# A hybrid decoder step in fp32: the SSD chunks' weight-times-value products and the token sums, each as two products of 64 stationary columns

## The reference, cut to what matters

```python
wgt = cbw[..., None] * lmask * dtb[:, None]
y = jnp.einsum('bijgr,bjgrp->bigrp', wgt, xb)          # per head: 128 tokens x 128 tokens, times 128 x 64
y = y + jnp.einsum('bign,bgrpn->bigrp', cb, s) * jnp.exp(cum)[..., None]
```

```python
y = xf * lax.rsqrt(jnp.mean(xf * xf, axis=-1, keepdims=True) + EPS)
```

## Time and profile before

| what | before |
|---|---|
| median of 3 runs | 2888.15 us (2887.59 to 2888.18) |
| profiled execution, its own time | 2894.47 us |
| its span | 2892.7 us |
| TensorE busy (PE) | 2830.8 us, 98% of the span |
| DVE, ACT, POOL busy | 58%, 20%, 35% |
| mean granted TensorE clock | 0.988 of full speed |

### The profile page before, as it was taken

The page is one execution under the profiler, slowest core; times in us unless marked ns, Lnnn a source line. Parts: engine busy times, 40 slices in busy tenths (PEclk is TensorE's granted clock), DMA queues, the critical chain, the costliest instruction groups (busy, mean ns, idle before and its releaser), DMA issues.

```text
span 2892.7 us, 46994 instructions
## 1 busy us (share of the span) xinstructions
PE 2830.8 (98%) x18230; PEld 2770.3 (96%) x18230; DVE 1667.6 (58%) x2116; ACT 589.2 (20%) x902; POOL 1020.8 (35%) x440
## 2 busy tenths in 40 slices
PE   9999999989999999999999999998999999999997
PEld 8999999989999999999999999998899999999997
DVE  7659786366444444444746597855664444444447
ACT  4333231113100011100323332211221110111102
POOL 2333233213344343443433333231144343443432
PEclk9999999999999999999999999999999999999998
DMA  4315324411111111111123334344011111111112
GB/s 157 129 67 165 119 99 163 133 53 38 52 44 48 47 44 51 44 48 46 56 89 100 119 123 145 108 140 140 31 46 44 51 44 51 44 44 51 44 51 86
DMA packets 76113, 228.08 MB, mean 79 GB/s; under 512 B 18704, under 2 KB 19728, under 8 KB 74912
## 3 DMA queue, kind: packets, MB, share of 16 engines
q1 hardware_dynamic: 71600, 210.79, 22.3%
q10 hardware_dynamic: 4368, 15.33, 1.8%
HBM read 180.63 MB, written 45.96 MB: 78 GB/s over the span
## 4 chain that ended last, share of the span: by engine, by line
PE 87%; issue 6%; DVE 5%; DMA 1%; POOL 1%; ACT 1%; DVEq 0%; SPq 0%; POOLq 0%; ACTq 0%
PE ps L696 27%; PE ps L698 26%; PE ps L697 26%; DVE sb_pt L1503 2%; PE ps L808 1%; PE ps L866 1%; DMA sb_w_raw<-w 1%; PE ps L810 1%; PE ps L929 1%; DMA sb_raw<-proj 0%; PE ps L813 0%; PE ps L930 0%; POOL sb_w_hi L675 0%; PE ps L974 0%; DVE sb_y_lo L1882 0%
## 5 line engine op out<-in xcount | busy, mean ns | idle before, releaser
L696 PE MATMUL ps<-sb_h_hi,sb_w_hi 128*128 128x344 f32 x3840 | 1244.0, 324 | 6.7 <-DVE sb_ev L1490 3.7
L697 PE MATMUL ps<-sb_h_lo,sb_w_hi 128*128 128x344 f32 x3840 | 1230.6, 320 | 0.0
L698 PE MATMUL ps<-sb_h_hi,sb_w_lo 128*128 128x344 f32 x3840 | 1230.1, 320 | 0.0
L675 POOL TENSOR_TENSOR sb_w_hi<-sb_w_raw,sb_ones 128x1024 fp32r<-128x1024 f32 x218 | 424.5, 1947 | 1813.3 <-PEq L693 861.5
L696 PEld LDWEIGHTS ps<-sb_h_hi,sb_w_hi 128*128 128x128 f32 x3840 | 726.2, 189 | 16.6 <-issue 7.5
L697 PEld LDWEIGHTS ps<-sb_h_lo,sb_w_hi 128*128 128x128 f32 x3840 | 726.2, 189 | 1.0
L698 PEld LDWEIGHTS ps<-sb_h_hi,sb_w_lo 128*128 128x128 f32 x3840 | 726.1, 189 | 0.0
L678 POOL TENSOR_TENSOR sb_w_lo<-sb_w_raw,sb_w_hi 128x1024 fp32r<-128x1024 f32 x218 | 596.1, 2734 | 17.1
L696 PE MATMUL ps<-sb_y_hi,sb_w_hi 128*128 128x344 f32 x1440 | 476.3, 331 | 20.7 <-DVE sb_x L1493 14.4
L698 PE MATMUL ps<-sb_y_hi,sb_w_lo 128*128 128x344 f32 x1440 | 465.4, 323 | 0.0
L697 PE MATMUL ps<-sb_y_lo,sb_w_hi 128*128 128x344 f32 x1440 | 462.7, 321 | 0.0
(11 more groups left out here) (266 smaller groups left out, 2256.4 us busy)
## 6 DMA issues: line engine op xcount, KB each, us to landing
sb_w_raw<-w SPq DMA_DIRECT2D x222, 512.0 KB, 3.6
proj<-sb_ev SPq DMA_DIRECT2D x64, 516.0 KB, 3.1
sb_pt<-proj SPq DMA_DIRECT2D x28, 516.0 KB, 5.1
sb_raw<-proj SPq DMA_DIRECT2D x16, 516.0 KB, 4.5
sb_raw<-proj ACTq DMA_DIRECT2D x16, 516.0 KB, 4.3
sb_ch<-cumT SPq DMA_DIRECT2D x32, 256.0 KB, 4.1
sb_raw<-ssd_state SPq DMA_DIRECT2D x4, 1024.0 KB, 6.4
o_ssd_s<-sb_ch SPq DMA_DIRECT2D x4, 1024.0 KB, 3.9
```

The source lines that it names most:

```text
L675: nc.gpsimd.tensor_tensor(w_hi[:, q, :], w_raw[:, q, :], ones[:, 0:1].to_broadcast([P, 1024]), ALU.mult).then_inc(sg.sem("w_hi_done"), 1)
L696: mm(o, wh, ah, start=first, stop=False)
L697: mm(o, wh, al, start=False, stop=False)
L698: return mm(o, wl, ah, start=False, stop=last)
```

## The change

Each 128-column stationary block of these products is halved. Where a product wrote 128 partitions of PSUM, there are now two: the first 64 stationary columns write partitions 0 to 63 and the other 64 write partitions 64 to 127, of the same bank and column. Both stream the same moving operand. The ninth product, that of the 8 sample tokens, stays one. No wait, buffer or transfer changes; the signal of the token sums still comes from the last product. In the "mix" call the early signal `w_used1` comes after the second half of the first block.

```diff
         def token_sums(key, freed=None):
 
-            for c in range(NCH + 1):
-                s = slice(c * CHUNK, min((c + 1) * CHUNK, T))
-                ins = mm(ps[0:s.stop - s.start, 7, c:c + 1], rstd[:, s], ones[:, 0:1], start=True, stop=True)
+            for c in range(NCH):
+                for n in range(2):
+                    s = slice(c * CHUNK + 64 * n, c * CHUNK + 64 * n + 64)
+                    ins = mm(ps[64 * n:64 * n + 64, 7, c:c + 1], rstd[:, s], ones[:, 0:1], start=True, stop=True)
                 if c == 0 and freed:
                     ins.then_inc(sg.sem(freed), 1)
-            ins.then_inc(*sg.on("tok_sum", key))
+            mm(ps[0:DEC, 7, NCH:NCH + 1], rstd[:, d], ones[:, 0:1], start=True, stop=True).then_inc(*sg.on("tok_sum", key))
@@
             for h in range(4):
-                mm(ps[:, 6, 64 * h:64 * h + 64], W(c)[:, 128 * h:128 * h + 128], xdt(c)[:, 64 * h:64 * h + 64],
-                   start=True, stop=True)
+                for n in range(2):
+                    mm(ps[64 * n:64 * n + 64, 6, 64 * h:64 * h + 64], W(c)[:, 128 * h + 64 * n:128 * h + 64 * n + 64],
+                       xdt(c)[:, 64 * h:64 * h + 64], start=True, stop=True)
@@
-        for c in range(NCH + 1):
-            s = slice(c * CHUNK, min((c + 1) * CHUNK, T))
-            ins = mm(ps[0:s.stop - s.start, 3, c:c + 1], ev[:, 1, s], ones[:, 0:1], start=True, stop=True)
-        ins.then_inc(*sg.on("tok_sum", "last"))
+        for c in range(NCH):
+            for n in range(2):
+                s = slice(c * CHUNK + 64 * n, c * CHUNK + 64 * n + 64)
+                mm(ps[64 * n:64 * n + 64, 3, c:c + 1], ev[:, 1, s], ones[:, 0:1], start=True, stop=True)
+        mm(ps[0:DEC, 3, NCH:NCH + 1], ev[:, 1, d], ones[:, 0:1], start=True, stop=True).then_inc(*sg.on("tok_sum", "last"))
```

## The result

The changed kernel took 2894.44 us (median of 20 runs, 2889.79 to 2896.20), the kernel before, beside it on the same chip, 2887.74 us (20 runs, 2884.25 to 2893.90). The ratio is 1.0019, with a 95% interval of 1.0013 to 1.0025: slower by 5.5 us (3.8 to 7.2), where 7.2 us of gain had been forecast. The two medians lie 6.7 us apart; the text goes by the ratio and its interval.

A forecast was written before the change was run, and what follows sets the result against it. TensorE, busy 98% of the span, was taken to bound the kernel. Gains of 4.6 (SSD steps) + 1.3 ("ffn") + 0.6 ("mix") + 0.7 (end) = 7.2 us gave 2881.0 us, range 2877.0 to 2885.8.

The forecast's parts named there:

- the one on "mix": Token sums of the "mix" calls: nothing arrives in the first layer, 0.64 us arrive in the second.
- The waits themselves should stay: SSD steps: TensorE's waits for DVE's last step or W(c) remain, because DVE starts on both from TensorE's earlier signal.
- SSD steps: Line 808's 32 steps: 0.07 us gained in each of 20 without a wait, 0.27 in 12 with one; 4.6 us.
- Every sign of being right: Expected timings at the changed products, about 12 waits as before, first "mix" spreading at about 42.93, last near DVE's reciprocal.
- "ffn": Token sums of the "ffn" calls, both layers: a projection product follows directly, so 2 x 0.64 = 1.3 us arrive.
- Of being wrong: Half loads spaced 0.055 us without overlap, longer SSD waits for DVE, or low-clock stretches changed by more than two.
- A pair of halves, the passage in: Halves load beside each other: sixteen loads take 0.62 us, and going from whole blocks to halves costs 0.25 us.
- The end: Last set of sums, line 1086: the final spreading starts earlier, at about 2874.0; gain 0.7 us, bounds 0 and 0.8.
- The rival on the clock: Clock falls come or go as work moves, 1.4 us each; two give 2878.2 or 2883.8 us; chance 0.28.
- serial halves: Halves load one after the other, so a round costs 0.11 us, not 0.06; 2898 us, 0.35% slower; chance 0.04.
- slow streams: Costlier passage in or halves' streams taking turns: sixteen loads 0.73 us or more, gain at most 3.7 us; chance 0.10.
- The rival that DVE takes the SSD gain: DVE sets the pace of SSD chunks, so line 808's waits grow; 2.6 us left, 2885.5 us; chance 0.10.

The follow-up runs named there:

- before_s32: The kernel before with 8 small products (8x8) added behind the warm-up and no halves anywhere; 2896.75 us, 1.0026 of the kernel before.
- after_w12: The changed kernel with a warm-up of 12 products of 208 columns in place of 20 of 128; 2886.59 us, 0.9993 of the kernel before.

## Why the prediction was wrong

The step that failed is the one on "mix": that the first layer's earlier end is idle time and that in the second layer "0.64 us arrive". The reading of the place itself held: the first layer's spreading starts at 42.99, still behind ACT's copy. Beyond it the prediction put the effect of the added instructions at nothing, without a reason: "The waits themselves should stay" is argued for the SSD steps alone. What it left out is that 32 more instructions stand ahead of everything behind them, and that TensorE's program is itself fetched through the DMA engines. It named no such rival: it asked only which of TensorE's own waits swallow a gain, and took the waits themselves for given. The runs put in its place, read in the two profiles: the fetch 3.4 us earlier, onto two stores (2.6 to 3.1 us become 3.8 to 3.9); DVE 1.1 us late; one more convolution step beside POOL; 3 us more wait in each layer where the wait would have been short; and a clock fall behind it. before_s32 shows this chain alone at 1.0026, after_w12 the change without it at 0.9993, and 1.0026 x 0.9993 = 1.0019, the measured ratio. As each is known to 0.001 only, the agreement to the last digit is luck; that the two add up to a loss is not.

The signs that the prediction named for itself are a lesson of their own. Every sign of being right came true: 0.55 to 0.58 us for the sixteen loads, 0.87 and 0.64 us to line 812, about 12 waits for DVE, 1.40 us for the sums of "ffn", the first spreading at 42.98, the last one 0.06 us behind the reciprocal. Of being wrong there was one faint sign, the idle time before the 12 SSD steps that wait, 5.5 us then and about 6.4 now (the 10.6 us in all 32 less 20 passages of 0.21); the list of low stretches has 15 entries against 14, and only their sum grew. All of them look at places that the change touches, and the loss arose elsewhere.

The other steps:

- **A pair of halves, the passage in** (0.25, then 0.62 for sixteen loads): right to 0.02 us.
- **SSD steps** (4.6 us): the mechanism right, the term too large. In steps like that at 303.40 the wait was to hide the whole passage of 0.25 us. It hides some 0.14 of it: the idle time in the bracket grew from 0.28 to 0.39 us. Line 810 has 12 waits for DVE, eight of them for the `sb_pt` step (line 1589), 1.9 us together. From line 812 of the unit's first chunk (265.96) to that of its seventh (304.04) it is 38.08 us; before, 303.66 less 265.08 is 38.58. Six steps gain 0.50 us, where 4 x 0.07 + 2 x 0.27 = 0.82 was forecast. With the units' first steps, four units gain about 3 us in all, by estimate.
- **"ffn"** (1.3 us): right, 0.65 us each.
- **The end** (0.7 us): the spreading does start 0.06 us after the reciprocal. But the forecast compared with an execution that ended late, and held the clock for given: behind the idle time that the halves open it is low to the end, in all five profiles with them. Against the mean of whole products the end is 0.3 us later (23.74 against 23.48 us).
- **What the halves leave**: 3 + 1.3 + 0.65 - 0.3 = 4.6 us should remain once the fetch is out of the way. after_w12 gains 2.0 us (between a gain of 4.6 and a loss of 0.6), so the difference lies just within the interval. The granted clock, though, is 0.9865 in its mean over the runs, against 0.988 for before. 0.0015 of 2890 us are 4.3 us of full clock, 8.7 us at half: a little of it is the end, which is at the low clock for some 21 us instead of 17 (in ten of the fifteen profiles with whole products; 19 in the other five). The rest are, by estimate, one or two more stretches in the middle, about 2 us, and what draws them there was not found.

The rival on the clock named the right price, 1.4 us, but not the cause: falls come behind waits that the change made. Nor did it have the size, since its worst case was 2883.8 us. The rivals on serial halves and slow streams fell with rows 271.60 and 701.02. The rival that DVE takes the SSD gain has a third of the gain of that part right.

## What to carry to other kernels

Products added to TensorE near its program's start moved a later fetch of that program in every kernel here, and a fetch is a 16 KB transfer among the kernel's own. Where a store or load is on the path, and the chain behind it ends in a race of two engines (here DVE's steps against POOL's split), 32 instructions cost 7 us here, and 32 more or fewer took it back. So read a change that only makes one engine's code longer against the DMA rows too, and try it with a few instructions more and fewer before judging it. Do not trust signs that look only at the places you changed. And be wary of speeding up the last thing ahead of a wait: it buys idle time, and in all five kernels that did it here the clock stayed low to the end.

## What was not expected of the hardware

- Two 516 KB stores whose data pass beside a 16 KB fetch of instructions land in 3.4 to 4.1 us instead of 2.6 to 3.2. The fetch alone is 2 to 3% of the DMA engines' time in that stretch, but it comes as one packet of 0.97 to 1.44 us: of the 16 parts of the first store fifteen land on time and one is 0.7 to 1.3 us late. The instruction that issues the second store takes 449 to 1022 ns instead of 324 to 332.
- The fetch moved forward by 3.4 to 3.6 us for the first 32 instructions, 3.8 us for 36 and 4.8 us for 48; a further 32 on top of 32 moved it by 2.4 to 2.6 us.
- DVE's convolution step takes 1.28 us, also where POOL starts in the middle of it, and 2.8 to 3.3 us when it starts while POOL splits weights. The outcome is nearly two-valued: with the first step up to 21.5 us behind the spreading the wait is 0.2 to 0.9 us, from 21.67 to 21.75 it is 3.15, and beyond 21.9 it is 3.3 to 4.1.
